# Chunk inversion in a gated delta rule: block transposes on VectorE, 128x32 and 128x64 tiles on TensorE, and squares of q and k on ScalarE

## The reference, cut to what matters

```python
lower = jnp.where(strict, jnp.einsum('bhncd,bhnsd->bhncs', kb, k) * decay, 0.0)
tinv = lax.linalg.triangular_solve(lower + eye, jnp.broadcast_to(eye, lower.shape), ...)
u = jnp.einsum('bhncs,bhnsv->bhncv', tinv, v * beta[..., None])
...
state = state * gt_i[..., None, None] + jnp.einsum('bhck,bhcv->bhkv', k_i, v_new)
```

## Time and profile before

| what | value |
|---|---|
| median of 3 runs | 1895.49 us (1892.24 to 1897.36) |
| the profiled execution's own time | 1895.78 us |
| its span | 1893.8 us |
| TensorE busy | 1811.6 us (96%) |
| VectorE busy | 1004.5 us (53%) |
| ScalarE busy | 645.8 us (34%) |
| GpSimd busy | 558.5 us (29%) |
| one pass of the loop | 67.36 us |

### The profile page before, as it was taken

The page is one execution under the profiler, slowest core; times in us unless marked ns, Lnnn a source line. Parts: engine busy times, 40 slices in busy tenths (PEclk is TensorE's granted clock), DMA queues, the critical chain, the costliest instruction groups (busy, mean ns, idle before and its releaser), DMA issues.

```text
span 1893.8 us, 29921 instructions
## 1 busy us (share of the span) xinstructions
PE 1811.6 (96%) x11609; PEld 1743.1 (92%) x11609; DVE 1004.5 (53%) x971; ACT 645.8 (34%) x1028; POOL 558.5 (29%) x492
## 2 busy tenths in 40 slices
PE   5999999987999999999996999999999999999997
PEld 5999999987999999999996989899999999999996
DVE  4477777762445445535545055645554554454556
ACT  6443333354344344335333253221222112122123
POOL 2344555423442333333240211121222212213120
PEclk9999999998999999999998999999999999999999
DMA  6132332323232422422338411111111111111112
GB/s 180 48 95 86 90 91 86 87 107 115 69 92 73 114 61 59 113 61 71 104 95 252 156 34 34 34 56 44 48 52 43 45 44 55 44 33 55 44 44 89
DMA packets 189848, 146.99 MB, mean 78 GB/s; under 512 B 22940, under 2 KB 178115, under 8 KB 188660
## 3 DMA queue, kind: packets, MB, share of 16 engines
q1 hardware_dynamic: 148740, 114.88, 20.8%
q10 hardware_dynamic: 40848, 31.49, 5.4%
q0 software_dynamic: 224, 0.12, 0.0%
HBM read 109.72 MB, written 36.74 MB: 77 GB/s over the span
## 4 chain that ended last, share of the span: by engine, by line
PE 83%; DVE 5%; issue 5%; DMA 2%; ACT 2%; POOLq 1%; DVEq 1%; POOL 1%; SPq 1%; ACTq 0%
PE gb L707 57%; PE db L970 12%; PE db L812 7%; PE db L809 3%; PE db L748 1%; DMA yo<-ot_d 1%; PE db L849 1%; PE db L848 1%; DVEq L1346 1%; DVE hx L1613 1%; POOLq L653 0%; PE db L923 0%; DVE fino L1719 0%; PE db L720 0%; ACT hx L1016 0%
## 5 line engine op out<-in xcount | busy, mean ns | idle before, releaser
L707 PE MATMUL gb<-u_hi,w_hi 128*128 128x342 f32 (+2 forms) x2520 | 827.1, 328 | 17.6 <-ACT ht L1255 7.3
L707 PE MATMUL gb<-u_lo,w_hi 128*128 128x342 f32 (+2 forms) x2520 | 812.2, 322 | 0.0
L707 PE MATMUL gb<-u_hi,w_lo 128*128 128x342 f32 (+2 forms) x2520 | 809.0, 321 | 0.0
L595 POOL TENSOR_TENSOR w_lo<-w_raw,w_hi 128x1024 fp32r<-128x1024 f32 x128 | 335.8, 2630 | 884.6 <-ACT w_hi L1012 884.6
L707 PEld LDWEIGHTS gb<-u_hi,w_hi 128*128 128x128 f32 x2520 | 479.9, 190 | 19.6 <-issue 18.0
L707 PEld LDWEIGHTS gb<-u_lo,w_hi 128*128 128x128 f32 x2520 | 480.0, 190 | 0.5
L707 PEld LDWEIGHTS gb<-u_hi,w_lo 128*128 128x128 f32 x2520 | 479.1, 190 | 0.0
L1390 DVE SCALAR_TENSOR_TENSOR cacc<-xb,prm,cacc 128x1040 f32<-128x1040 f32 x72 | 174.3, 2421 | 11.2 <-issue 10.5
L1685 DVE TENSOR_TENSOR h<-h,db 128x512 f32<-128x512 f32 x176 | 117.1, 685 | 57.4 <-PE db L970 57.0
L970 PE MATMUL db<-w_hi,a_hi 128*128 128x512 f32 x352 | 140.2, 398 | 3.4 <-DVE a_lo L1709 2.9
L1012 ACT ACTIVATE w_hi<-w_raw 128x1024 fp32r<-128x1024 f32 x128 | 133.6, 1052 | 18.7 <-ACT tm L1077 17.3
(11 more groups left out here) (218 smaller groups left out, 2104.7 us busy)
## 6 DMA issues: line engine op xcount, KB each, us to landing
w_raw<-in_w_in SPq DMA_DIRECT2D x53, 512.0 KB, 3.9
w_raw<-in_w_up SPq DMA_DIRECT2D x44, 512.0 KB, 3.7
qkv_d<-tm ACTq DMA_DIRECT2D x24, 576.0 KB, 3.1
tk<-qkv_d SPq DMA_DIRECT2D x9, 1536.0 KB, 7.7
w_raw<-in_w_down SPq DMA_DIRECT2D x22, 512.0 KB, 3.3
ot_d<-ots ACTq DMA_DIRECT2D x9, 512.0 KB, 3.2
yb_d<-ybs ACTq DMA_DIRECT2D x8, 513.0 KB, 3.8
yl<-yb_d SPq DMA_DIRECT2D x8, 513.0 KB, 5.2
```

The lines of the kernel that those rows point to most:

```text
L595: pool.tensor_tensor(w_lo[:, n % SLOTS, :], w_raw[:, n % SLOTS, :], w_hi[:, n % SLOTS, :].bitcast(F32), ALU.subtract).then_inc(s_wlo, 1)
L707: mm = pe.matmul(gb[:, bank, 0:w], wt, u, start=(k == 0 and m == 0), stop=(k == KT - 1 and m == 2))
```

## The change: what it does

1. The transposes TT0, T0 and T1 leave TensorE, and their copies leave ScalarE. VectorE makes them with a transpose of 32x32 squares from SBUF to SBUF: `rr` from `bd` (128x1024), and `tt_m` from `rr` after Y0 (two of 128x512). That is enough because after level 0 all that is filled lies in 32x32 squares on the diagonal.
2. X1 and Y1 compute only the 32x32 squares that level 1 fills: two matmuls a head for X1, three for Y1 (the third gives the transposed square, in place of T1). VectorE copies the squares out with smaller instructions and without a mask.
3. X2 and Y2 compute one 64x64 square a head. Even heads write to PSUM partitions 0 to 63, odd heads to 64 to 127, and VectorE takes them out separately.
4. `FILLS` is dealt anew: GROW 1 (was 3), OT 5 (was 2), Y0 2 (was 1), X1 1 (was 0).
5. In stage one the squares move from GpSimd to ScalarE, which reads PSUM, and they and the sums are left out for v.

The core of the diff:

```diff
 REC = ["P1", "V", "O", "SU", "OT"]
-STEPS = ["P1", ... "TQD", "OT", "TT0"]
+STEPS = ["P1", ... "TQD", "OT"]
...
-FILLS = {"P1": 2, "TKN": 0, "V": 1, "TKB": 0, "GROW": 3, "KK": 2, "TQ": 2, "TKG": 2, "O": 2, "SU": 2, "QK": 1,
-         "TQD": 1, "OT": 2, "TT0": 1, "X0": 1, "Y0": 1, "T0": 1, "X1": 0, "Y1": 1, "T1": 1, "X2": 0, "Y2": 1}
+FILLS = {"P1": 2, "TKN": 0, "V": 1, "TKB": 0, "GROW": 1, "KK": 2, "TQ": 2, "TKG": 2, "O": 2, "SU": 2, "QK": 1,
+         "TQD": 1, "OT": 5, "X0": 1, "Y0": 2, "X1": 1, "Y1": 1, "X2": 0, "Y2": 1}
...
@@ GpSimd
-                pool.wait_ge(s_tm, 3 * i + j + 1)
-                if j > 0:
-                    pool.wait_ge(s_ssq, 3 * i + j)
-                pool.tensor_tensor(sq[:, :, :], tm[:, :, :], tm[:, :, :], ALU.mult).then_inc(s_sq, 1)
...
@@ TensorE
+                elif name == "X1":
+                    def left_squares(o, m):
+                        for z in (0, HALF):
+                            t = pe.matmul(o[z + SQ:z + HALF, 0:SQ], at_m[:, m, z + SQ:z + HALF], tt_m[:, m, z:z + SQ],
+                                          start=True, stop=True)
+                        return t
+                    each([(s_tt, 2 * (c - 1))], left_squares)
+                elif name == "Y1":
+                    def right_squares(o, m):
+                        for z in (0, HALF):
+                            pe.matmul(o[z:z + SQ, 0:SQ], nmx[:, m, z:z + SQ], rr[:, m, z + SQ:z + HALF],
+                                      start=True, stop=True)
+                        return pe.matmul(o[SQ:HALF, 0:SQ], rr[:, m, SQ:HALF], nmx[:, m, 0:SQ], start=True, stop=True)
+                    each([done["X1"], done["Y0"]], right_squares)
+                elif name == TOP_X:
+                    each([done["Y1"]], lambda o, m: pe.matmul(
+                        o[side(m), 0:HALF], at_m[:, m, HALF:], tt_m[:, m, 0:HALF], start=True, stop=True))
+                elif name == LAST_Y:
+                    each([done[TOP_X]], lambda o, m: pe.matmul(
+                        o[side(m), 0:HALF], nmx[:, m, 0:HALF], rr[:, m, HALF:], start=True, stop=True))
...
@@ ScalarE
+                    if squared:
+                        q = act.activation(sq[:, c0:c1, :].rearrange("p c d -> p (c d)"), db[:, r, 0:(c1 - c0) * P],
+                                           ACT.Square)
                     t = act.activation(tm[:, c0:c1, :].rearrange("p c d -> p (c d)"), db[:, r, 0:(c1 - c0) * P],
                                        ACT.Copy)
...
@@ VectorE
                 if q == 0:
-                    sums(QKV_TILES - 1)
                     cumulate()
...
+                elif name == TOP_X:
+                    for h in range(2):
+                        dve.wait_ge(s_ps[name], 2 * (c - 1) + h + 1)
+                        for m in range(2):
+                            t = dve.tensor_copy(heads(nmx, h)[HALF:, m::2, 0:HALF],
+                                                dbank(name, h)[side(m), m::2, 0:HALF])
+                        t.then_inc(s_ev[name], 1)
...
+                elif name == "Y0":
+                    for h in range(2):
+                        dve.wait_ge(s_ps[name], 2 * (c - 1) + h + 1)
+                        dve.tensor_tensor(heads(rr, h), heads(rr, h), dbank(name, h), ALU.subtract).then_inc(s_ev[name], 1)
+                        drain()
+                        turned_squares(heads(tt_m, h), heads(rr, h)).then_inc(s_tt, 1)
```

More of the change, by code:

```diff
@@ L116 @@
 REC = ["P1", "V", "O", "SU", "OT"]
-STEPS = ["P1", "TKN", "V", "TKB", "GROW", "KK", "TQ", "TKG", "O", "SU", "QK", "TQD", "OT", "TT0"]
-DOUBLING = ["TT0"]
+STEPS = ["P1", "TKN", "V", "TKB", "GROW", "KK", "TQ", "TKG", "O", "SU", "QK", "TQD", "OT"]
+DOUBLING = []
 for _n in range(len(LEVELS)):
-    DOUBLING += [f"X{_n}", f"Y{_n}"] + ([f"T{_n}"] if _n < len(LEVELS) - 1 else [])
-STEPS += DOUBLING[1:]
+    DOUBLING += [f"X{_n}", f"Y{_n}"]
+STEPS += DOUBLING
 LAST_Y = DOUBLING[-1]
+TOP_X = DOUBLING[-2]
+HALF = CH // 2
+SQ = CH // 4
+assert LEVELS == [SQ // 2, SQ, HALF] and SQ == 32
 PREP_STEPS = [s for s in STEPS if s not in REC and s not in DOUBLING]
@@ L827, in step @@
                     each([done["TQ"]], product(knt, qnt))
-                elif name == "TT0":
+                elif name == "X0":
                     pe.wait_ge(s_bd, 16 + 16 * BLKS * c)
[L831 to L834, removed]
+                    each([done["KK"]], product(at_m, bd))
                 elif name == "Y0":
[L836 to L840, removed]
+                    pe.wait_ge(s_rr, c)
+                    each([done["X0"]], product(nmx, rr))
+                elif name == "X1":
[18 more added lines that the diff above has]
+                        o[side(m), 0:HALF], nmx[:, m, 0:HALF], rr[:, m, HALF:], start=True, stop=True))
                 elif name == "P1":
@@ L1102, in _ @@
                 qkv_tile(j)
-            with act.Fori(0, QKV_TILES // 3 - 1) as i:
+            with act.Fori(0, 4) as i:
                 for j in range(3, 6):
                     qkv_tile(j, i)
+            for j in range(15, 18):
+                qkv_tile(j, squared=j <= 2 * HEADS)
+            with act.Fori(0, 2) as i:
+                for j in range(18, 21):
+                    qkv_tile(j, i, False)
             def exponentials():
@@ L1194, in _ @@
                     act_step(name, 0)
-            for h in range(2):
-                act.wait_ge(s_ps["TT0"], h + 1)
-                act.activation(heads(rr, h), dbank("TT0", h), ACT.Copy).then_inc(s_ev[LAST_Y], 1)
             def gates(u, i):
@@ L1400, in _ @@
             conv(0, 0)
[L1401 removed]
+            with dve.Fori(0, 5) as i:
                 for j in range(3):
@@ L1404, in _ @@
                     sums(3 * i + j)
-            for n in (QKV_TILES - 2, QKV_TILES - 1):
-                conv(n, n % 3)
-                sums(n - 1)
+            conv(16, 16 % 3)
+            sums(15)
+            with dve.Fori(0, 2) as i:
+                for j in range(3):
+                    conv(17 + 3 * i + j, (17 + j) % 3)
+            conv(QKV_TILES - 1, (QKV_TILES - 1) % 3)
             def by_chunk(m):
```

77 lines of the change are left out of this document (52 added, 25 removed).

## The result

The changed kernel takes 1843.2 us (median of 4 runs, 1842.46 to 1844.31) against 1896.42 us (4 runs, 1892.24 to 1898.61): a ratio of 0.9722, 95% interval 0.9704 to 0.9741. In a later comparison on another chip it took 1845.05 us, 0.9728 (0.9713 to 0.9742). The forecast was 1876 us in a range from 1850 to 1893.

A forecast was written before the change was run, and what follows sets the result against it. TensorE was taken to bound stage one and the loop, a chain through other engines stage two. Per pass 10.19 us go and 8.04 come: 17.2 us over eight, plus 2.5 in stage two, giving 1876 us (bounds 1864 to 1889, range 1850 to 1893).

The forecast's parts named there:

- I take 0.0625 us: Price of each of 112 small records a pass in X1, Y1, X2 and Y2: 7.00 us a pass.
- faster records: Rival: small records cost what their columns scale to, 0.028 and 0.056 us; 5.1 us less a pass, 1852 us; chance 0.13.
- the second figure: Skill's about 25 ns a small matmul if the hardware decodes it: records sum to 2.80 us a pass instead of 7.00.
- Changes of tile: TensorE switches between full and column tiles six times a pass at 0.09 us: 0.54 us (0 to 1.7).
- X2, Y2 and the wait: Y2 starts 1.48 us after X2, whose records end at 1.00 us: 0.5 us of waiting a pass (0.3 to 1.3).
- What leaves: TT0, T0, T1 (2.61 us) and X1 with Y1, X2 with Y2 (7.58 us) leave TensorE: 10.19 us a pass.
- (a): VectorE's two transposes between Y0 and X1 cost nothing; halves may last 2.6 and 1.45 us; disturbed, about 0.3 us a pass.
- no change: Rival: TensorE waits for transposes, small copies and tile changes, 2.9 us a pass against 2.15 saved; 1890 to 1899 us; chance 0.09.
- (b): Transpose of `bd` costs nothing: `bd` is there 1.2 us before X0, VectorE's copy not needed before Y0.
- (c): Squares on ScalarE in stage one cost nothing: 1.5 us a tile for 16 tiles, engine busy 109 of 286 us.
- (d): After the doubling, P1, then TKN, waits for VectorE's form 5.6 us in eight passes; that chain stays.
- Stage two: VectorE's pool sums no longer slowed by GpSimd's squares: next tile at some 375 instead of 377.27, 2.5 us less.

The follow-up runs named there:

- experiment 2: Changed kernel with both 32x32 squares of a head in X1 written to the same PSUM partitions 32 to 63 (one column tile): 1847.82 us, ratio 0.9755.
- experiment 3: Changed kernel with X1 loading all 128 columns of at_m as weights and still multiplying 32 columns: 1870.68 us, ratio 0.9869.
- experiment 1: Changed kernel with all heads of X2 and Y2 writing to PSUM partitions 0 to 63 (one column tile): 1846.72 us, ratio 0.9742.
- experiment 9: Changed kernel with one piece of the projection moved from behind OT to between X2 and Y2: 1838.86 us, ratio 0.9701.
- experiment 5: Changed kernel with X2 and Y2 as full 128 by 128 products again, with VectorE's mask and subtraction as before: 1854.37 us, ratio 0.9776.
- experiment 6: Changed kernel with the 24 transposes of a pass put back on TensorE as mere load, VectorE keeping its own: 1862.67 us, ratio 0.9814.
- experiment 7: Changed kernel with each of VectorE's two transposes between Y0 and X1 made twice: 1853.59 us, ratio 0.978.
- experiment 8: Changed kernel with the squares back on GpSimd, and VectorE's sums for v and ahead of the cumulated sums again: 1847.95 us, ratio 0.9744.

## Why the prediction was wrong

**The step that failed is the price of a small record, "I take 0.0625 us".** For X1 and Y1 the sum had (32 + 48) x 0.0625 = 5.00 us a pass; measured are 0.63 + 0.64 = 1.27, with the way into the tiles. That is 3.73 us a pass and 29.8 us in eight, of the 30.9 us by which the loop's gain exceeded the forecast (48.1 - 17.2). The row from which it came has loads of 128 columns, 16 rows high, with 16 multiplied. It is the price of neither side: with 128 rows a record costs 0.032 us at 32 columns and 0.110 us as soon as 128 are loaded (experiments 2 and 3). The trace of before has a second run of this kind, transposes with 2 rows and 2 columns multiplied:

```profile
1096.48 0.65 PE L923 MATMUL db<-cst,hx 2*128 2x2 f32 x8 [0.33 <-DVE hx L1613]
```

A record lasts 0.20 us, so eight start within 0.45 us, 0.064 us apart, as with 16 columns. So the multiplied columns didn't set the pace of the row, and a price for few columns couldn't be read from it. Why it is 0.0625 and not 0.110 with 128 columns loaded no run shows; the few rows are what these two runs have in common. The prediction saw that "loads of 128 columns in rows 5 may set the 0.0625 us" and gave that rival 0.13.

Nor do the bounds hold what failed. The forecast's 1864 to 1889 us vary the tile changes, the waits and the small VectorE work, and the terms shown for the first two alone span some 1870 to 1892. The price of a record, the one term read from a row of another kind, is not varied in them.

**The rival "faster records" had the right direction and half of the mechanism.** It scaled a record with its columns, 0.028 and 0.056 us, which is near what a record costs where one tile is in use (0.032 and 0.058, experiments 2 and 1). What no case had is that records for different column tiles run side by side: two tiles in X1 and X2, three in Y1. The Trainium skill, TensorEngine Tiling (Array Packing), section Key Properties, says that different tiles can execute loads and multiplies in parallel. By that rule X1 would cost half of what it costs in one tile; the trace agrees for the records (0.016 against 0.032 us apart) and not quite for the step (0.63 against 1.13 us), which holds the way into the tiles too. I had read that section for its line on draining and not for this one.

**Against a second rule the measurement decides.** The Trainium skill, TensorE: Matmul & The Clock Gate, section "Wait — 56ns, not 53.3ns?", has 62 ns a matmul, or a floor of about 25 ns however small. Here records start 16 ns apart in two column tiles and 11 ns in three: with several column tiles neither figure is a floor. The prediction put the second figure beside its sum (2.80 us) and gave it no chance. With it the prediction's own sum gives 8 x (10.19 - 2.80 - 1.04) + 2.5 = 53.3 us less, 1842.5 us, an estimate by that page's figure. That it meets the measured 1843.2 is luck: no group of records ran at 25 ns, some ran faster (16 and 11) and some slower (29 to 58), and the wait and the tile changes were larger than in the sum.

**Changes of tile.** Forecast six at 0.09, 0.54 us a pass. The chain shows 0.20 us at each of three returns to the full array, 0.60 us, and has the way in inside the groups. Counted beyond the pace of the records, a group costs some 0.3 us for both ways (experiment 2), some 0.9 us a pass. So the forecast was low, inside its bounds of 0 to 1.7.

**X2, Y2 and the wait.** Forecast 1.48 + 1.00 = 2.48 us, measured 2.24. The small copies take 0.28 us as estimated. TensorE waits 0.55 and 0.17 us, not 0.5, since the records are shorter than forecast; this wait has in part taken the place of the records removed, and experiment 9 gets it back.

**What leaves.** Experiments 5 and 6 split the 6.06 us of a pass: 2.57 the transposes, 1.37 X2 and Y2, and 2.12 remain. No run puts X1 and Y1 back; the rows give for them 3.79 - 1.27 - 0.40 = 2.12, so the remainder is theirs. "10.19 us" of work that leaves was right.

**Edits costed at nothing.** (a) The transposes: 0.71 us each, with no wait ahead of X1. The limits moved with the record price: X1's second half is due 0.32 us after its first and not 1.0, so the cover is thinner than forecast (experiment 7). For the bad case the prediction had 0.3 us here and some 1 us in its rival "no change", and shows no working for the second. (b) `bd`: no wait of TensorE ahead of X0 or Y0 in the loop. (c) ScalarE is busy for 124.79 instead of 109.30 us of stage one, and TensorE still has no gap. (d) P1 and TKN's wait for VectorE's form: 6.4 us in nine, against the 5.6 of the earlier trace rows.

**Stage two.** Forecast 2.5 us. The second pool tile starts at 375.38, forecast "at some 375 instead of 377.27", for the reason given: VectorE's copy ahead of it now waits 3.35 us for TensorE. The starts of whole executions differ by up to 1.7 us here (373.64 in the second profile of the changed kernel), so the distance from the first tile says more: 14.20 us in both, 16.68 before, 2.5 us less. To the first P1 it was 1.6 us in the one pair of profiles, and 2.8 over all of them (experiment 8).

## What to carry to other kernels

For float32 records that use all 128 rows, as here, price a small matmul by the wider of its loaded and multiplied columns (0.032 us at 32, 0.058 at 64, 0.110 at 128), divided by the number of column tiles that neighbouring records alternate between. In a loop that TensorE fills, cutting full products down to the blocks that aren't zero and spreading them over different column tiles took X1 from 1.78 to 0.83 us with its return, and X2 with Y2 from 3.79 to 2.44. What remains is set by the waits between dependent steps and by some 0.3 us for each group's way into column tiles and back. Before taking a price from the nearest row, compare both widths and the rows in use, and look for a second row that differs in one of them: the row here had 16 rows, 128 columns loaded and 16 multiplied, and its price fits neither width of a record with 128 rows.

## What the runs showed of the hardware that I had not expected

- Records of different column tiles overlap: they start 0.016 us apart with two tiles and 0.011 with three, against 0.032 in one (32 columns wide).
- Loaded and multiplied columns weigh alike: 128 loaded with 32 multiplied costs 0.110 us a record in the full array, and 32 loaded with 128 multiplied 0.054 in two alternating tiles.
- A run of 32 such records (3.5 us) with full loads and 32 columns multiplied was followed by a granted clock of 0.50 from 632 to 634 us, though TensorE had no gap. Six of the seven passes seen of this kernel took 1.4 to 3.0 us more than the first, at a mean granted clock of 0.95 to 0.97; the first kept 1.00.
- GpSimd's squares slow VectorE all through stage one: the convolution's steps take 1.51 us in the mean without them and 2.42 with them (below: experiment 8, then the changed kernel). TensorE hides it there; in stage two, together with the last sums moved out of the way, it is worth the 2.5 us.

```profile
L1407 DVE SCALAR_TENSOR_TENSOR cacc<-xb,prm,cacc 128x1040 f32<-128x1040 f32 x72 | 174.2, 2420 | 11.2 <-issue 10.6
```

```profile
L1410 DVE SCALAR_TENSOR_TENSOR cacc<-xb,prm,cacc 128x1040 f32<-128x1040 f32 x72 | 109.0, 1514 | 11.3 <-issue 10.6
```

- Left open: whether `st` could be zeroed ahead of the first substitution, where GpSimd waits some 10 us. It shares its place with `ybs`, whose last store starts at 429.3 us, so other places would be needed. The same holds for making `kd` there too: it shares its place with `p_hi`, which TensorE still reads then. Neither was measured.
